# Later waits for last stores, first weights ahead of constants, and heads loaded in pieces, in a five-stage transformer layer

## The reference

```python
h = rms_norm(x, norm_mix_g)
qa, ka, va, qb, kb, vb, gates = split(h @ w_in)
ya = swa_sink_attention(qa, ka, va, ...)          # chunks of 64, window 128, QK-norm, bias, sinks
yb = stick_breaking_attention(qb, kb, vb)         # 8 heads of 64
#   A[t,s] = sig(z_ts) * prod_{s<j<t} (1 - sig(z_tj)), s < t;  yb = A @ vb
gate = sigmoid(gates + b_gate)                    # 2 x 1024 channels
x = x + (gate[0] * (ya @ w_proj_a) + gate[1] * (yb @ w_proj_b)) @ w_out
x = x + hierarchical_moe(rms_norm(x, norm_ffn_g)) # top-1 of 4 groups, top-2 of its 8 SwiGLU experts
```

## Time and profile before

| | |
|---|---|
| median of 3 runs | 2780.48 us (2779.88 to 2785.07) |
| the profiled execution | 2781.56 us, its span 2779.7 us |
| PE, DVE, ACT, POOL busy | 2607.9, 1636.7, 1491.0, 602.5 us |
| granted TensorE clock, mean | 0.97 |
| bytes moved | 536.66 MB, 193 GB/s in the mean |

### The profile page before, as it was taken

One profiled execution on the slowest core, in us unless ns is written; L12 is line 12 of the kernel. 1 busy time (PEld: TensorE's weight loads), 2 busy tenths in 40 slices (PEclk: granted clock), 3 DMA queues, 4 the chain that ended last, 5 costly groups with the idle time before them and its releaser, 6 DMA issues. The chain is left out here.

```text
span 2779.7 us, 41171 instructions
## 1 busy us (share of the span) xinstructions
PE 2607.9 (94%) x13541; PEld 2158.9 (78%) x13542; DVE 1636.7 (59%) x2207; ACT 1491.0 (54%) x2640; POOL 602.5 (22%) x706
## 2 busy tenths in 40 slices
PE   7899899869999999899799999669999999999997
PEld 6787677658887887788679999558788888888886
DVE  4401455358777776677543333479766667766673
ACT  4312676457766666666422122338666667756563
POOL 0000111035444444344000000012222112212121
PEclk9999999989999999999889999879999999999999
DMA  6454334576456635623554343469977778866783
GB/s 181 119 201 150 111 121 132 159 257 203 179 177 210 203 139 165 206 102 118 178 162 135 120 136 104 154 220 384 363 241 240 227 233 319 319 226 227 226 300 75
DMA packets 196352, 536.66 MB, mean 193 GB/s; under 512 B 19928, under 2 KB 70552, under 8 KB 191744
## 3 DMA queue, kind: packets, MB, share of 16 engines
q1 hardware_dynamic: 169616, 432.80, 45.1%
q0 software_dynamic: 26608, 102.17, 13.3%
HBM read 403.36 MB, written 131.53 MB: 192 GB/s over the span
## 5 line engine op out<-in xcount | busy, mean ns | idle before, releaser
L1064 POOL TENSOR_TENSOR sb_sig<-sb_sig,sb_R 128x512 f32<-128x512 f32 (+1 forms) x320 | 340.7, 1065 | 456.6 <-DVE sb_R L1012 456.5
L51 PE MATMUL ex_ps_h<-ex_wu_hi,ex_x_hi 128*128 128x512 f32 x816 | 323.6, 397 | 2.4 <-DVE ex_x_lo L1817 2.4
L53 PE MATMUL ex_ps_h<-ex_wu_hi,ex_x_lo 128*128 128x512 f32 x816 | 319.3, 391 | 0.0
L52 PE MATMUL ex_ps_h<-ex_wu_lo,ex_x_hi 128*128 128x512 f32 x816 | 318.2, 390 | 0.0
L1822 DVE TENSOR_TENSOR ex_wu_lo<-ex_w,ex_wu_hi 128x1024 fp32r<-128x1024 f32 x248 | 285.3, 1216 | 2.6 <-ACT ex_wu_hi L1678 2.2
L1012 DVE TENSOR_TENSOR_SCAN sb_R<-sb_z,sb_R,sb_zeros 128x512 f32<-128x512 f32 x192 | 245.6, 1279 | 56.4 <-ACT sb_z L936 56.0
L1827 DVE TENSOR_TENSOR ex_wd_lo<-ex_w,ex_wd_hi 128x1024 fp32r<-128x1024 f32 x200 | 239.6, 1219 | 51.1 <-ACT ex_wd_hi L1685 51.0
L945 ACT CAST sb_aT_hi<-sb_pst 128x512 fp32r<-128x512 f32 (+1 forms) x320 | 168.3, 526 | 158.7 <-PE sb_pst L1093 155.6
L1678 ACT CAST ex_wu_hi<-ex_w 128x1024 fp32r<-128x1024 f32 x248 | 241.3, 1055 | 10.9 <-DMA ex_w<-in_w_exp 10.0
L1020 DVE TENSOR_TENSOR sb_aT_lo<-sb_pst,sb_aT_hi 128x512 fp32r<-128x512 f32 (+1 forms) x320 | 192.2, 601 | 76.2 <-ACT sb_aT_hi L945 73.7
L935 ACT ACTIVATE sb_sig<-sb_z 128x512 f32<-128x512 f32 (+1 forms) x320 | 172.4, 539 | 88.0 <-PE sb_z L1086 86.6
(11 more groups left out here) (270 smaller groups left out, 6318.1 us busy)
## 6 DMA issues: line engine op xcount, KB each, us to landing
ex_w<-in_w_exp SPq DMA_DIRECT2D x384, 512.0 KB, 9.1
sb_w_hi<-wg_d SPq DMA_DIRECT2D x48, 512.0 KB, 3.6
sb_w_lo<-wg_d SPq DMA_DIRECT2D x48, 512.0 KB, 4.6
gates<-sb_go SPq DMA_DIRECT2D x64, 256.0 KB, 3.0
mo_gates<-gates SPq DMA_DIRECT2D x64, 256.0 KB, 3.6
h<-mo_rows POOLq DMA_DIRECT2D x17, 512.0 KB, 3.0
nt_x<-in_x SPq DMA_DIRECT2D x16, 512.0 KB, 4.5
vhl<-nt_vo SPq DMA_DIRECT2D x16, 512.0 KB, 5.5
```

The source lines that it names most:

```text
L51: nc.tensor.matmul(out, w_hi, x_hi, start=first, stop=False)
L52: nc.tensor.matmul(out, w_hi, x_lo, start=False, stop=False)
L53: return nc.tensor.matmul(out, w_lo, x_hi, start=False, stop=last)
L1064: nc.gpsimd.tensor_tensor(sig[:, j % 5, 0:width], sig[:, j % 5, 0:width], R[:, r, first:first + width], ALU.mult).then_inc(a_done, 1)
```

## The change

The waits for the last stores of stages 1, 2 and 3 (`vhl`; `yaT`; `ybT` and `gates`) are moved from the end of the stage to places in the next one: the semaphores are made in `build` and passed to both. Stage 1 has two semaphores for its constants, and takes token tile 0 ahead of weight quarter 1. In stage 2 the first weight tile is rounded and split in two halves, the table load goes behind the first tiles, and ACT and DVE do `rstd(1)`, `exps(0)` and `norms(1)` ahead of `take(FIRST + 1)` and `take_low(FIRST + 1)`. In stage 3 the table load and DVE's constants go behind the first two weight tiles, weight tile 2 and the kept copy of tile 0 are issued ahead of the values of head 0, and heads 1 to 7 are loaded in six pieces, three steps apart, from step 7 of the head before on, with the values at step 25. Stores of gates come at `item_end + 2` and of y at `+ 3`. The diff, cut (a line of dots stands for what is left out):

```diff
 def norm_and_values(...):                       # stored is now a parameter, in all four stages likewise
@@ sync
             load_x(0)
-            sp.dma_start(g_bc[:, :], g.partition_broadcast(P)).then_inc(const_in, 16)
-            sp.dma_start(ident[:, :], ident_d).then_inc(const_in, 16)
+            sp.dma_start(g_bc[:, :], g.partition_broadcast(P)).then_inc(g_in, 16)
+            sp.dma_start(ident[:, :], ident_d).then_inc(ident_in, 16)
...
-            for u in range(2):
-                sp.wait_ge(stored[u], NT // 2 * 16)
@@ scalar
             round_wv(0)
+            take_hi(0)
             round_wv(1)
-            take_hi(0)
@@ vector
-            dve.wait_ge(const_in, 32)
...
                 dve.wait_ge(rstd_ready, n + 1)
+                if n == 0:
+                    dve.wait_ge(g_in, 16)
...
             split_wv(0)
+            take_lo(0)
             split_wv(1)
-            take_lo(0)
@@ tensor
-            pe.wait_ge(const_in, 32)
+            pe.wait_ge(ident_in, 16)
 def projection_and_banded_attention(...):       # ba_o is moved to the front of the SBUF tensors
@@ sync (ahead of the constants; POOL has the same wait ahead of the bias reads, DVE ahead of the eps memset)
+            for u in range(2):
+                sp.wait_ge(vhl_stored[u], NT // 2 * 16)
...
-                sp.wait_ge(o_stored[u], N // 2 * 16)
@@ scalar
-            nc.scalar.preload_act_table(ACT.Ln)
...
-            round_w(0)
+            act.wait_ge(w_in[0], 16)
+            nc.scalar.copy(wh[:, 0, 0:KD // 2, :], w[:, 0, 0:KD // 2, :]).then_inc(first_rounded, 1)
+            nc.scalar.copy(wh[:, 0, KD // 2:KD, :], w[:, 0, KD // 2:KD, :]).then_inc(w_rounded, 1)
             round_w(1)
+            nc.scalar.preload_act_table(ACT.Ln)
...
             squares(1)
-            take(FIRST + 1)
             rstd(1)
             exps(0)
+            take(FIRST + 1)
@@ vector
-            split_w(0)
+            dve.wait_ge(first_rounded, 1)
+            nc.vector.tensor_tensor(wl[:, 0, 0:KD // 2, :], w[:, 0, 0:KD // 2, :], wh[:, 0, 0:KD // 2, :],
+                                    ALU.subtract).then_inc(first_split, 1)
+            dve.wait_ge(w_rounded, 1)
+            nc.vector.tensor_tensor(wl[:, 0, KD // 2:KD, :], w[:, 0, KD // 2:KD, :], wh[:, 0, KD // 2:KD, :],
+                                    ALU.subtract).then_inc(w_split, 1)
...
+            norms(1)
             take_low(FIRST + 1)
-            norms(1)
@@ tensor, half_unit
+                if m == 0 and h == 0:
+                    pe.wait_ge(first_split, 1)
+                if m == 0 and h == 1:
+                    pe.wait_ge(w_split, 1)
 def stick_breaking_and_gates(...):
@@ sync; load_head takes parts=range(6) and issues those of its six transfers
             load_head(0, slice(TC, S))
+            load_w(2)
+            keep_w(0)
             load_v(0)
-            keep_w(0)
-            load_w(2)
+            load_w(3)
             keep_w(1)
-            load_w(3)
-            load_head(1)
-            load_v(1)
-            load_h(KP)
-            load_h(KP + 1)
-            for j in range(NSTEP + 2):
+            for j in range(NSTEP + 4):
                 for it in range(NI):
-                    if j == item_end(it) + 1:
+                    if j == item_end(it) + 2:
                         store_gate(it)
...
+                for g in range(KP, HSLOTS):
+                    if j == item_end(2 * (g - KP) + 6):
+                        load_h(g)
...
-                    if j == (item_end((t - 1) * NG + 6) if kp < 2 else pair_end(t * NG - 1, kp - 2)):
+                    if j == (item_end((t - 1) * NG + 2 * kp + 6) if kp < 2 else pair_end(t * NG - 1, kp - 2)):
                         load_h(g)
                 if j == item_end(NG + 2):
                     sp.wait_ge(w_split, 2 * NG)
+                    for u in range(2):
+                        sp.wait_ge(ya_stored[u], NT // 2 * 16)
...
-                    if j == 4 * q + PROD + 1:
+                    if j == 4 * q + PROD + 3:
                         store_y(n)
-                for h in range(HB - 2):
-                    if j == (h + 1) * UH:
-                        unit(sp, z_done, (h + 1) * UH - 1)
-                        load_head(h + 2)
-                    if j == (h + 1) * UH + 5:
-                        sp.wait_ge(quad_done, QH * (h + 1))
-                        load_v(h + 2)
-            for b in range(2):
-                sp.wait_ge(stored[b], HB // 2 * NC_ * 16)
-            for b in range(2):
-                sp.wait_ge(g_stored[b], NI // 2 * 16)
+                for h in range(1, HB):
+                    if j == (h - 1) * UH + 7 and h > 1:
+                        unit(sp, z_done, (h - 1) * UH - 1)
+                    for i in range(6):
+                        if j == (h - 1) * UH + 7 + 3 * i:
+                            load_head(h, parts=(i,))
+                    if j == (h - 1) * UH + 25:
+                        if h > 1:
+                            sp.wait_ge(quad_done, QH * (h - 1))
+                        load_v(h)
@@ scalar: the Sigmoid table load goes behind round_w of tiles 0 and 1; take_hi(0) waits for ya_stored
@@ vector: the wait for const_in, nident, mask, the four memsets and their waits go behind split_w of tiles 0 and 1
@@ tensor: pe.wait_ge(prep, 1) goes from the start of the stage to scores(0)
 def merge_and_output_projection(...):
@@ sync, ahead of the first loads; the last two stores are waited for at chunk NCH - 2
+            for b in range(2):
+                sp.wait_ge(yb_stored[b], (HB // 2 * NC_ - 1) * 16)
+                sp.wait_ge(gates_stored[b], (NG * NC_ // 2 - 1) * 16)
```

More of the change, by code:

```diff
@@ L610, in _ @@
             dve.wait_ge(bias_in, 32)
+            for u in range(2):
+                dve.wait_ge(vhl_stored[u], NT // 2 * 16)
+            nc.vector.memset(eps[:, :], EPS).then_inc(prep, 1)
             chain(nc.vector.tensor_copy(bias_end[:, :, :], bias[:, :, :]))
@@ L833, in _, with load_head @@
         def _(sp):
-            def load_head(h, cols=slice(0, S)):
+            def load_head(h, cols=slice(0, S), parts=range(6)):
                 u, t = h % 2, h // 2
@@ L837, in load_head @@
                 done = first_in if cols.stop == TC else head_in[u]
-                for dst, rows, src, tile in (
-                        (qs, 0, qk_hi, t), (qs, HD, qk_lo, t), (kh, 0, qk_hi, t + 4), (kh, HD, qk_hi, t + 4),
-                        (kl, 0, qk_lo, t + 4), (kl, HD, qk_lo, t + 4)):
+                whole = ((qs, 0, qk_hi, t), (qs, HD, qk_lo, t), (kh, 0, qk_hi, t + 4), (kh, HD, qk_hi, t + 4),
+                         (kl, 0, qk_lo, t + 4), (kl, HD, qk_lo, t + 4))
+                for i in parts:
+                    dst, rows, src, tile = whole[i]
                     sp.dma_start(dst[rows:rows + HD, u, cols].bitcast(F32), src[tile, half, cols]).then_inc(done, 16)
@@ L942, in take_hi @@
                 unit(act, turned, j)
+                if j == 0:
+                    for u in range(2):
+                        act.wait_ge(ya_stored[u], NT // 2 * 16)
                 if r == 0 and q >= 2:
@@ L974, in _ @@
                     round_w(n, pc)
+            nc.scalar.preload_act_table(ACT.Sigmoid)
             for j in range(NSTEP + 2):
@@ L992, in _ @@
         def _(dve):
-            dve.wait_ge(const_in, 48)
-            nc.vector.tensor_copy(nident[:, :], stage[:, 0, :])
-            nc.vector.tensor_copy(mask[:, :], stage[:, 1, :]).then_inc(prep, 1)
-            for r in range(4):
-                nc.vector.memset(R[:, r, r * P:r * P + 1], 1.0).then_inc(prep, 1)
-            dve.wait_ge(zeros_set, 1)
-            dve.wait_ge(prep, 5)
             def scan(j):
@@ L1037, in _ @@
                     split_w(n, pc)
+            dve.wait_ge(const_in, 48)
+            nc.vector.tensor_copy(nident[:, :], stage[:, 0, :])
+            nc.vector.tensor_copy(mask[:, :], stage[:, 1, :]).then_inc(prep, 1)
+            for r in range(4):
+                nc.vector.memset(R[:, r, r * P:r * P + 1], 1.0).then_inc(prep, 1)
+            dve.wait_ge(zeros_set, 1)
+            dve.wait_ge(prep, 5)
             for j in range(NSTEP + 2):
@@ L1074, in scores @@
                 if j == 0:
+                    pe.wait_ge(prep, 1)
                     pe.wait_ge(first_in, 96)
@@ L1146, in merge_and_output_projection @@
 def merge_and_output_projection(nc, yaT, ybT, gates, wp_tiles, wo_d, x, g2, wr_d, ident_d, h2_d, out, logits, cst_d, cst, b_all, b_bc,
-                                stage, w_in):
+                                stage, w_in, yb_stored, gates_stored):
     CT = 2 * P
```

39 lines of the change are left out of this document (21 added, 18 removed).

## The result

| | before | after |
|---|---|---|
| median of the runs on one chip | 2780.74 us (4 runs, 2779.88 to 2785.07) | 2722.27 us (4 runs, 2720.67 to 2723.42) |
| ratio of after to before | | 0.9782, 95% interval 0.977 to 0.9794 |
| profiled execution, span | 2781.56, 2779.7 | 2722.95, 2721.1 |

Predicted were 2722.5 us, range 2709 to 2743.

A forecast was written before the change was run, and what follows sets the result against it. TensorE, busy 94% of the span, was taken to bound the kernel through its waits and half-clock stretches. Gains 5.6 + 9.0 + 21.0 + 21.3 + 1.7 - 0.5 = 58.1 us gave 2722.5 us, range 2709 to 2743.

The forecast's parts named there:

- Part 1: Stage ends: SyncE no longer waits there for three stages' last stores: 6.0 us gained, 1.8 of it counted within Part 4.
- Part 2: Second stage's start: first weights in halves, table load behind them, with 2.5 of Part 1: 5.6 us gained.
- Part 3: Block 1 of the second stage: exponentials and norms ahead of a projection tile remove PE's 7.4 us wait: 9.0 gained.
- Part 4: Third stage's start: 1.8 from the earlier block start, 16.7 from weight tile 4's wait, 2.5 slow clock: 21.0 us gained.
- Rival (b): Third stage: head loads run as fast as other tiles, 421 GB/s, so ACT resumes 7.5 us sooner: 2715; chance 0.08.
- Part 5: Third stage: heads in six pieces end PE's waits for gate-weight read-backs and a gate store: 21.3 us gained.
- Rival (d): Third stage: every head piece delays a read-back without slack, PE losing 75 us against 58 gained: 2798; chance 0.03.
- Rival (a): Third stage: the queue still starves weight tile 4 or 5; Part 4 gives 12, Part 5 loses 3: 2735; chance 0.17.
- Parts 6 and 7: Output stage's start: 1.7 us gained from the moved store wait. First stage's new order: 0.5 us lost.

The follow-up runs named there:

- experiment 3: The changed kernel with SyncE waiting for the last stores at the ends of stages 1, 2 and 3 again: 2726.96 us, ratio 0.9796.
- experiment 10: The changed kernel with the second stage's first weight tile rounded and split whole instead of in halves: 2722.3 us, ratio 0.978.
- Experiment 5: The changed kernel with the projection tile taken ahead of the norms and exponentials of block 1 again: 2729.73 us, ratio 0.9815.
- experiment 2: The changed kernel with head 1, its values and two activation pairs issued at stage 3's start again: 2740.82 us, ratio 0.985.
- experiment 8: The kernel before with only the head loads changed (heads 1 to 7 in pieces, head 1, values and activations later): 2738.12 us, ratio 0.9833.
- experiment 6: The changed kernel with stage 3's start in the old order: values 0, kept copy 0, tile 2, kept copy 1, tile 3: 2723.39 us, ratio 0.979.
- experiment 4: The changed kernel with ACT's table load and DVE's constants ahead of stage 3's first weights again: 2720.66 us, ratio 0.9779.
- experiment 9: The changed kernel with head 0 in three cuts, weight tiles 2 and 3 and kept copies between them, values last: 2721.44 us, ratio 0.979.
- experiment 7: The changed kernel with weight quarter 1 rounded and split ahead of token tile 0 in stage 1 again: 2721.13 us, ratio 0.9782.
- experiment 11: The changed kernel with head 0 in three cuts and gate-weight tile 4 rounded and split three steps later: 2720.46 us, ratio 0.9773.
- experiment 1: The changed kernel with heads 2 to 7 loaded whole in bursts at the old steps again: 2746.68 us, ratio 0.9864.

## Why the prediction was right, by its steps

**Part 1 (6.0).** Right in its size: experiment 3 puts 6.1 on the three waits. But "tens of microseconds after landing" is not true of the first one. In stage 2 SP meets the wait for `vhl` at the very start and stands 2.2 us there in after:

```profile
SPq L371 <- DMA vhl<-nt_vo: 2.2, 1, 2.2
```

It costs PE nothing, since only loads of constants stand behind it, and no wait of PE names them. The other new waits show nowhere.

**Part 2 (5.6).** The boundary and the halves came as worked out: 4.85 against 4.8. The term that was mis-sized is the clock. I took half of a 1.5 us gain, on the ground that a gap of 3.6 us might be too short to bring it down. It did come down, and PE did 6.0 us of its work at the low clock (129.21 to 135.20) where before did 3.1, so that the term measured -1.4 and not +0.75. The length of the gap alone does not decide this: in experiment 10 it was 4.5 us, and the low stretch ended 3.8 us after PE began. I should have given this term a spread of 2 us both ways and no value.

**Part 3 (9.0).** Measured 7.8. The wait went but for 0.39 us, and that rest has a cause in the working: "with the first table already loaded" was wrong. The table load stands behind the wait for the sums in the new order too, so the chain from the sums to the keys took 5.8 us (274.18 to 279.97) and not 4.5.

```profile
274.18 1.28 ACT L469 ACT_TABLE_LOAD   x1 [1.58 <-PE ba_ps_kv L676]
```

The slow clock was worth 1.7, as said (1.8). The rest of the error is a term that I put at nothing, what comes late behind the exponentials: right behind block 1 after loses 0.9 us again, at the sums of the next block (284.45) and at the probabilities (286.15). So 7.0 + 1.7 - 0.9 = 7.8. Experiment 5 has 8.5, since its work at the low clock was longer, 5.35 us against the 3.7 of the earlier trace rows, and cost 2.4.

**Part 4 (21.0).** Tile 4: 19.2 predicted and 19.2, 19.4, 19.2 measured (after, experiments 2 and 8). ACT found the tile landed, as the sum of 1.84 MB said: it landed at 556.5 (issued at 548.49, row below), 4.5 us behind the kept copy of tile 1 where 4.4 was predicted, and ACT asked for it at 558.18.

```profile
w_stage<-in_w_gate SPq DMA_DIRECT2D x1, 512.0 KB, 8.0
```

The step that failed is "the queue sets the time at which ACT resumes, and it moves only by the earlier block start", with its 7.3 MB up to tile 3. PE's fifth unit needs only the sigmoids behind tile 2, which ACT does before it asks for tile 3, and in after tile 2 may be rounded when tile 0's kept copy has landed. Tile 3, 6.65 us later, was hidden. The earlier trace rows had this already: the fifth unit of before starts at 562.36, ahead of tile 3's 565.31. With the values no longer ahead, ACT resumed 1.3 us sooner than the block start alone would give (559.32 to 545.45, less the 10.78 gained before the stage and the 1.8), and 0.55 more came from less work at the low clock behind it: together the 1.85 by which this term was too small (experiment 6: 2.6 for this order). I had seen that "tile 2 now lies ahead of the values" and put it aside. Not counting PE's 7 us earlier start was right (experiment 4).

Rival (b) was wrong on the speed. Three stretches of after, with only head 0 in the queue, with only a kept copy, and with only the values:

```profile
533.00:539.00 6.00, 6.00 (x33) 4.66 (x31) 1.22 (x1) 0.70 (x2) 1.30 (x1) 1.00 1.02 226
```

```profile
542.90:545.30 2.40, 0.00 (x0) 0.00 (x0) 0.00 (x0) 0.00 (x0) 0.00 (x0) 0.50 1.04 435
```

```profile
545.40:547.75 2.35, 0.00 (x0) 0.00 (x0) 1.65 (x3) 2.30 (x6) 0.00 (x0) 0.50 0.99 408
```

The third is the load of values 0, also 128 partitions, so the difference is not one of loads against stores. At full share the 64-partition loads move 226 GB/s, the 128-partition stores 435 and the 128-partition load 408. The Trainium skill (SBUF — State Buffer, Door 1: The DMA port swizzle) has a reason that fits, and that I missed when I took its DMA page to mean that halves cost no more per byte: bandwidth goes by how many of 16 ports the partitions reach, and partitions 0 to 63 reach eight. An estimate from its 435 GB/s is 218, and the trace agrees to 4% (226). No run here changes the number of partitions alone.

**Part 5 (21.3).** 22.6 in the ledger, 22.7 in experiment 8. No read-back took over 6.1 us, under the 7.3 I had bounded a piece's delay by. Rival (d), that some 30 pieces would each meet a read-back without slack, fails on this. Rival (a) fails in after too, but experiment 9 shows how near it is: once PE comes 8 us sooner, tile 4 is late by 6.

**Parts 6 and 7** came as said (1.6 and -0.5). For part 7 that is no confirmation: kernels with the same first stage differ by more at its end (experiment 7).

**Not predicted:** 1.5 us within stage 4 and -0.8 in stage 5, which the change does not touch there. PE's waits for `mo_wo_lo` are 10.6 us before, 8.1 in after, and 8.3 to 10.9 in other kernels here, and those that have after's stage 4 pass it from 1.7 us faster to 0.7 slower than after. So I read this as spread between executions and not as an effect. It, part 5 and part 4's start (+4.6 together) cancelled the clock, block 1 and stage 5 (-4.1). That the total is 0.2 us from the median is luck.

## What to carry to other kernels

Where a queue serves transfers in order, read which landing each in-order engine asks for next, and put ahead of it only what is asked for before; big loads with tens of microseconds of slack belong in pieces behind the small urgent ones, and here that was 42 of 58 us. When such a wait is removed, look at what that engine asks for next in its queue: twice here (experiments 9 and 11) the gain stopped at the next tile. A wait for a last store belongs with its first reader, since the barrier does not ask for it.

## What the runs showed of the hardware that I had not expected

**The same code after the same gap can run at half clock for different times.** Experiment 9 has after's code up to stage 3 and the same wait of 3.5 us at the start of stage 2. After worked at 0.50 for the 6.0 us from its first matmul at 129.21 to 135.20; experiment 9 at 0.61 in the mean over 4.3 us from 128.38 to 132.71. Its stretch from 132 to 135, beside after's above (0.50, x9):

```profile
132.00:135.00 3.00, 3.00 (x13) 2.41 (x12) 0.00 (x0) 0.00 (x0) 0.00 (x0) 0.88 0.19 44
```

That is 1.2 us in one place. Stages 1, 2 and 5 each show such jumps, 1.2 to 3.4 us, between kernels that are alike there, which is why single profiles differ by 3 to 4 us. A term under 2 us can be read from one of them only as a step at one place (a wait that comes or goes, as in experiment 3), not as a difference over a stage.

**What a wait costs beyond its length** differed even for waits of one length: 7.41 us cost 1.7 more in before and 2.4 more in experiment 5. It was 2.2 us for 17.2 (experiment 2) and 7.5 for 17.0 in three waits (experiment 1).
